# Moving 18 gathered dot products into the routing stage, and letting VectorE's weight remainders lead by two blocks

## The reference, cut to what matters

```python
def chunk_fn(hc):                                   # 128 tokens at a time
    q = (hc @ w_query).reshape(PEER_CHUNK, PEER_HEADS, PEER_KEY_DIM)     # 8 heads
    s1 = jnp.einsum('chk,nk->chn', q[..., :PEER_HALF_DIM], keys_1)       # 128 keys
    s2 = jnp.einsum('chk,nk->chn', q[..., PEER_HALF_DIM:], keys_2)
    v1, i1 = lax.top_k(s1, PEER_TOPK_HALF)                               # 16 of 128
    v2, i2 = lax.top_k(s2, PEER_TOPK_HALF)
    cand = (v1[..., :, None] + v2[..., None, :]).reshape(PEER_CHUNK, PEER_HEADS, -1)
    cand_idx = (i1[..., :, None] * N_KEYS + i2[..., None, :]).reshape(PEER_CHUNK, PEER_HEADS, -1)
    top_s, pos = lax.top_k(cand, PEER_TOPK)                              # 16 of 256
    experts = jnp.take_along_axis(cand_idx, pos, axis=-1)                # of 16384
    gate = jax.nn.softmax(top_s.astype(jnp.float32), axis=-1).astype(hc.dtype)
    u = jnp.take(expert_u, experts, axis=0)
    act = jax.nn.gelu(jnp.einsum('chkd,cd->chk', u, hc))
    v = jnp.take(expert_v, experts, axis=0)
    return jnp.einsum('chk,chkd->cd', gate * act, v)
```

## Time and profile before

| what | us |
|---|---|
| median of three runs (lowest, highest) | 2969.31 (2959.89, 2971.57) |
| the profiled execution, its own time | 2977.3 |
| its span in the trace | 2975.5 |
| PE busy | 2872.6 (97%) |
| DVE busy | 1737.5 (58%) |
| POOL busy | 1257.9 (42%) |
| ACT busy | 1114.3 (37%) |

### The profile page before, as it was taken

The page is one execution under the profiler, slowest core; times in us unless marked ns, Lnnn a source line. Parts: engine busy times, 40 slices in busy tenths (PEclk is TensorE's granted clock), DMA queues, the critical chain, the costliest instruction groups (busy, mean ns, idle before and its releaser), DMA issues. The chain is left out here.

```text
span 2975.5 us, 42156 instructions
## 1 busy us (share of the span) xinstructions
PE 2872.6 (97%) x14606; PEld 2452.6 (82%) x14606; DVE 1737.5 (58%) x2980; ACT 1114.3 (37%) x1499; POOL 1257.9 (42%) x1348
## 2 busy tenths in 40 slices
PE   7899999999999999999999999999996899999998
PEld 5777888877688878787789999999985799999997
DVE  7957555234445541797507995877732456666664
ACT  5554222236442223424334334656641223333332
POOL 2635777554157765686455775111100020122210
PEclk9999999999999999999999999999997999999999
DMA  8315555522045553232233555888872677788772
GB/s 335 120 37 212 197 191 167 159 87 89 27 137 197 193 177 109 86 102 72 84 105 113 157 155 161 289 285 283 284 250 80 222 265 269 273 289 289 274 258 83
DMA packets 184380, 532.75 MB, mean 179 GB/s; under 512 B 17376, under 2 KB 79584, under 8 KB 182496
## 3 DMA queue, kind: packets, MB, share of 16 engines
q1 hardware_dynamic: 143584, 402.44, 40.7%
q0 software_dynamic: 18432, 67.12, 7.1%
q10 hardware_dynamic: 22272, 61.98, 5.5%
HBM read 470.65 MB, written 60.82 MB: 179 GB/s over the span
## 5 line engine op out<-in xcount | busy, mean ns | idle before, releaser
L615 POOL TENSOR_TENSOR w_lo<-raw,w_hi 128x256 fp32r<-128x256 f32 x1216 | 1112.9, 948 | 729.0 <-ACT w_hi L652 727.9
L2000 PE MATMUL ps<-h_hi,w_hi 128*128 128x512 f32 (+1 forms) x2392 | 925.4, 387 | 51.4 <-DVE w_lo L1901 38.7
L2000 PE MATMUL ps<-h_hi,w_lo 128*128 128x512 f32 (+1 forms) x2392 | 914.9, 382 | 0.0
L2000 PE MATMUL ps<-h_lo,w_hi 128*128 128x512 f32 (+1 forms) x2392 | 893.9, 382 | 0.0
L652 ACT ACTIVATE w_hi<-raw 128x1024 fp32r<-128x1024 f32 x509 | 538.9, 1060 | 901.8 <-PE ps L2000 636.4
L2000 PEld LDWEIGHTS ps<-h_hi,w_hi 128*128 128x128 f32 x2392 | 455.6, 190 | 131.7 <-issue 50.8
L2000 PEld LDWEIGHTS ps<-h_hi,w_lo 128*128 128x128 f32 x2392 | 455.1, 190 | 69.9 <-issue 0.2
L2000 PEld LDWEIGHTS ps<-h_lo,w_hi 128*128 128x128 f32 x2392 | 455.2, 190 | 69.0 <-issue 0.7
L633 POOL DMA_INDIRECT t_row<-in_u_rows,t_ix x64 | 64.9, 1013 | 540.0 <-DVE t_dot L1908 535.1
L1901 DVE TENSOR_TENSOR w_lo<-raw,w_hi 128x1024 fp32r<-128x1024 f32 x200 | 243.6, 1219 | 52.0 <-ACT w_hi L652 50.5
L1263 DVE CUSTOM_DVE_ANT_0 ada<-ada,cvec 128x1024 f32<-128x1024 f32 x144 | 225.3, 1594 | 30.7 <-DMA ada<-in_ada 26.0
(11 more groups left out here) (384 smaller groups left out, 3850.1 us busy)
## 6 DMA issues: line engine op xcount, KB each, us to landing
ada<-in_ada SPq DMA_DIRECT2D x144, 512.0 KB, 3.6
raw<-in_expert_u SPq DMA_DIRECT2D x128, 512.0 KB
raw<-in_expert_v SPq DMA_DIRECT2D x128, 512.0 KB
raw<-in_ffn_in SPq DMA_DIRECT2D x88, 512.0 KB
expert_act<-g_act ACTq DMA_DIRECT2D x128, 224.0 KB, 4.2
gate_matrix<-w_st ACTq DMA_DIRECT2D x14, 2048.0 KB, 8.6
e_w<-gate_matrix SPq DMA_DIRECT2D x16, 1792.0 KB
e_g<-expert_act SPq DMA_DIRECT2D x128, 224.0 KB
```

The costliest lines, as they stand in the source:

```text
L615: last = nc.gpsimd.tensor_tensor(w_lo[:, k, c:c + 256], raw[:, k, c:c + 256], w_hi[:, k, c:c + 256].bitcast(F32), ALU.subtract)
L2000: return nc.tensor.matmul(out, a, b, start=start, stop=stop_)
```

## The change

It has four parts.

1. **Early dots.** The row numbers of the first 64 tokens are made right after tile 0 of the routing (those tokens lie in it). 18 of the 64 dots move into the routing: one follows every third step from step 24 on (`E_STEP`; tile 1 begins with step 23). Their gathers stand in POOL's program behind every second split, from U block 18 on (`E_BLOCK`), in three buffers `t_early` of their own. The transposes and the copy that make `t_h` move from U block 52 to behind U block 3. The routing loop is written out instead of looped.
2. **Fewer dots later.** In the gates stage 1/2 dot per block instead of 3/4, in the last 16 U blocks 1/2 instead of 1/4, the last 10 in the first 10 V blocks; V rows start at V block 16, 5/8 of one per block, fewer of them in the first block of a group.
3. **Remainders lead.** In the last 16 U blocks iteration b writes remainders up to block b+2 before it does `gated`; at the first V block of each group the remainder of the V block two ahead comes before `e_t`, and so do that iteration's dots and rows.
4. **SP.** The fourth V block's raw load and group 1's `e_w` stand before the wait for the last activations, and that `e_w` waits only for the last `e_t` of group 0.

```diff
+EARLY, E_BLOCK, E_STEP = 18, 18, 24
+    t_early = [ar(f"t_early{i}", (8 + 4 * i) * K, [D]) for i in range(U_SLOTS)]
...
-        for k in range(2):
-            sp.wait_ge(act_st[k], ADA_ALL + 16 * NK // 2)
-        with sp.Fori(0, NG - 1) as g:
+        def group_step(g):
             for k in range(GE):
                 sp_raw(sp, (g * GE + (mv + k + 3), (mv + k + 3) % RING), A["expert_v"][g * GE + (k + 3), :, :], 1024)
                 if k == 0:
                     gates_in(g + 1)
+                    if isinstance(g, int):
+                        for b in range(2):
+                            sp.wait_ge(act_st[b], ADA_ALL + 16 * NK // 2)
                 group_in(g + 1, k)
+        group_step(0)
+        with sp.Fori(1, NG - 1) as g:
+            group_step(g)
...
-    V_DOTS = 32
+    V_DOTS = 16
+    SHARE = (0, 3, 4, 5, 6, 7, 8, 9)
+    def front(v):
+        return v // GE * GE + GE * SHARE[v % GE] / 10
     def dots_by(b):
-        if b < U_GATES:
-            return max(0, b) * 3 // 4
         if b < U_BLOCKS:
-            return U_GATES * 3 // 4 + (b - U_GATES) // 4
-        return min(ROWS, U_GATES * 3 // 4 + U_LAST // 4 + (b - U_BLOCKS) * 5 // 8)
+            return EARLY + max(0, b) // 2
+        return min(ROWS, EARLY + U_BLOCKS // 2 + int(front(b - U_BLOCKS)))
     def rows_by(v):
-        return min(ROWS, max(0, v - V_DOTS) * 3 // 4)
+        return min(ROWS, int(front(max(0, v - V_DOTS)) * 5 / 8))
...
+        pool.wait_ge(row_ready, 2)
+        for m in range(first * RING, gates):
             split(m, m % RING)
-        pool.wait_ge(row_ready, 2)
+            b = m - M0["expert_u"] - E_BLOCK
+            if b >= 0 and b % 2 == 0 and b // 2 < EARLY:
+                gather(b // 2)
+        pool.wait_ge(row_ready, 3)
         pool.wait_ge(rt_mm, 1)
+        for j in range(EARLY, ROWS):
+            gather(j)
...
         def step(ins):
             own_d.link(dve, ins)
+            taken["steps"] += 1
+            if taken["steps"] >= E_STEP and taken["steps"] % 3 == 0 and taken["dots"] < EARLY:
+                if taken["dots"] == 0:
+                    dve.wait_ge(row_ready, 2)
+                    dve.wait_ge(row_copied, 1)
+                dve_dot(dve, taken["dots"])
+                taken["dots"] += 1
...
-        with dve.Fori(0, TT) as i:
+        for i in range(TT):
...
+            if i == 0:
+                for a in range(PKS):
+                    rows, picks = slice(a * GT, (a + 1) * GT), slice(a * ROWS, (a + 1) * ROWS)
+                    last = v.scalar_tensor_tensor(out=t_dot[rows, :], in0=r_i[0:GT, 0, 0, picks], scalar=float(NK),
+                                                  in1=r_i[0:GT, 1, 0, picks], op0=ALU.mult, op1=ALU.add)
+                step(last)
+                v.tensor_copy(t_ix[:, :], t_dot[:, :]).then_inc(row_ready, 1)
...
-        for b in range(U_GATES, U_BLOCKS):
-            dve_remainder(dve, gates + b - 1)
-            if b == U_BLOCKS - GE:
+        def remainders(b):
+            while ahead[0] < b:
+                dve_remainder(dve, gates + U_GATES + ahead[0])
+                ahead[0] += 1
...
+        for b in range(U_LAST):
+            remainders(b + min(3, b + 1))
+            if b == U_LAST - GE:
...
+                def lead():
+                    remainders(U_LAST + n + 3)
+                def work():
+                    dots(U_BLOCKS + n)
+                    rows(n)
+                if k == 0:
+                    lead()
+                    work()
+                    gated(g + 1, k, (g + 1) % 2, lambda: None)
+                else:
+                    gated(g + 1, k, (g + 1) % 2, lead)
+                    work()
```

More of the change, by code:

```diff
@@ L556, in gates_in @@
         def gates_in(g):
-            if not isinstance(g, int):
+            if not isinstance(g, int) or g:
                 sp.wait_ge(wa_t, g * GE)
@@ L622, in pool_program, with gather @@
         gates = M0["expert_u"] + U_FIRST
-        with pool.Fori(2, gates // RING) as i:
+        first = (M0["expert_u"] + E_BLOCK) // RING
+        def gather(j):
+            if j >= U_SLOTS:
+                pool.wait_ge(row_used, j - U_SLOTS + 1)
+            nc.gpsimd.indirect_dma_start(out=row_slot(j)[:, :], out_offset=None, in_=A["u_rows"],
+                                         in_offset=bass.IndirectOffsetOnAxis(ap=t_ix[:, j:j + 1], axis=0))\
+              .then_inc(u_in[j % U_SLOTS], 16)
+        with pool.Fori(2, first) as i:
             for k in range(RING):
                 split(i * RING + k, k)
-        for m in range(gates // RING * RING, gates):
+        pool.wait_ge(row_ready, 2)
+        for m in range(first * RING, gates):
             split(m, m % RING)
-        pool.wait_ge(row_ready, 2)
+            b = m - M0["expert_u"] - E_BLOCK
+            if b >= 0 and b % 2 == 0 and b // 2 < EARLY:
+                gather(b // 2)
+        pool.wait_ge(row_ready, 3)
         pool.wait_ge(rt_mm, 1)
[L630 to L635, removed]
+        for j in range(EARLY, ROWS):
+            gather(j)
         pool.wait_ge(blk_done, M0["expert_v"])
@@ L1137, in act_peer @@
         four(0)
+        act.wait_ge(row_mm, 1)
+        nc.scalar.activation(t_h[:, :].rearrange("p (b n) -> p b n", b=2), pa[:, 0:2, :], ACT.Copy).then_inc(row_copied, 1)
         with act.Fori(1, U_FIRST // RING - 1) as i:
@@ L1819, in dve_router @@
         v = nc.vector
+        taken = {"steps": 0, "dots": 0}
         def step(ins):
             own_d.link(dve, ins)
+            taken["steps"] += 1
[5 more added lines that the diff above has]
+                taken["dots"] += 1
         def settle(ins):
@@ L1862, in dve_router @@
         v.tensor_tensor(e, e, bc(z1, 2, TK), ALU.mult).then_inc(gate_done, 1)
+        assert taken["dots"] == EARLY
         dve.wait_ge(gate_done, 1)
         for a in range(PKS):
[L1865 to L1870 removed]
+            last = v.tensor_copy(t_gate[a * GT:(a + 1) * GT, :], r_i[0:GT, 2, 0, a * ROWS:(a + 1) * ROWS])
+        last.then_inc(row_ready, 1)
         v.tensor_copy(iota_t[:, :, :], bc(iota, 2, 2))
@@ L1904, in dve_dot @@
     def dve_dot(dve, j):
-        row = t_row[j % U_SLOTS]
+        row = row_slot(j)
         dve.wait_ge(u_in[j % U_SLOTS], 16 * (j // U_SLOTS + 1))
@@ L2416, in pe_peer @@
         m, T = M0["expert_u"], T0["expert_u"]
-        with pe.Fori(0, U_FIRST // RING - 1) as i:
-            for k in range(RING):
-                first(m, T, k, i, RING)
+        for k in range(RING):
+            first(m, T, k, 0, RING)
         pe.wait_ge(row_ready, 1)
@@ L2423, in pe_peer @@
         last.then_inc(row_mm, 1)
+        with pe.Fori(1, U_FIRST // RING - 1) as i:
+            for k in range(RING):
+                first(m, T, k, i, RING)
         for k in range(U_FIRST - RING, U_FIRST - RING // 2):
```

67 lines of the change are left out of this document (28 added, 39 removed).

## The result

The changed kernel takes 2930.31 us (median of four runs, 2923.99 to 2934.16) against 2964.73 us for the kernel before (four runs, 2959.89 to 2971.57): ratio 0.988, 95% interval 0.9847 to 0.9913. That is 1.2% faster, by 34.4 us and clear of noise, inside the range of the forecast and 6.9 us above its 2923.4. The profiled execution took 2926.46 us with a span of 2924.7, 50.8 us less than the profiled one of before (2977.3).

A forecast was written before the change was run, and what follows sets the result against it. PE bounds the kernel, so time is won only where it idles or runs at its lower clock. -57.5 - 9.5 + 18.7 + 2.4 = -45.9 us from a median of 2969.3 gives 2923.4; own range 2911 to 2941, stated range 2905 to 2942.

The forecast's parts named there:

- Ring of U blocks 120 to 127: Waits circling remainder, PE, gelu, `wa_hi`, `wa_lo`; leading remainders open it, eight blocks take 39.0 us instead of 96.5: gain 57.5.
- Stage border: V group 0 takes 39.7 us instead of 49.2, with the remainder before `e_t` and `e_w` issued earlier: gain 9.5.
- Fewer dots in the gates stage: Gates stage: PE has no idle time there that a freer DVE could give back: 0 us.
- V rows per group: V stage: rows from block 16, 5/8 per block, and dots in the first V blocks cost 0 us.
- the slower rival: V groups: a row waiting for its gather delays `wa_lo` in 13 groups; 3 us past the slack gives 2994 us; 3%.
- Stall at the transposes: Routing's end: dots wait for gathers tied to PE, so PE stands still 18.7 us; floor 12.8, ceiling 25.
- POOL's lag: Splits 35 to 39: POOL falls 3 to 6 us behind, mostly made up before block 52; full at last gather 2929, 8%.
- Clock after the stall: PE restarts at the lower clock after standing still at the routing's end: loss 2.4 us, ends 0 and 5.
- The `t_h` transposes ahead of PE's loop: Transposes and copy moved ahead make block 52's split end 1 us later; no other cost counted.
- The rival without a stall: Routing's end: gathers land well ahead, 21.6 us of dots fit in 26.15 us of slack, time 2902 us; 5%.
- another wait takes the ring's place: U blocks 120 to 127: queued `e_g` loads or ACT's order keep half of the 67.0 us, time 2957; 7%.
- The rule of the Trainium skill: Two-input VectorE instructions and GpSimd SBUF reads exclude each other; each of 18 dots costs POOL up to its own length.

The follow-up runs named there:

- sp_old: `lead_only` with SP's wait for the last activations ahead of group 0 again, as before the change: median 2909.56 us, lowest 2903.07, ratio 0.9817.
- lead_only: Changed kernel without early dots (EARLY = 0), later dots and V rows spread as in the kernel before: median 2897.65 us, lowest 2896.02, ratio 0.9764.
- th_late: `lead_only` with the `t_h` transposes and ACT's copy behind U block 51 again, PE's loop from block 0: median 2894.81 us, lowest 2892.27, ratio 0.976.
- step30_block15: Changed kernel with early dots from routing step 30 instead of 24 and gathers from U block 15 instead of 18: median 2902.42 us, lowest 2899.01, ratio 0.9778.
- lead_one: `lead_only` with remainders in U blocks 112 to 127 one iteration earlier than before the change, instead of three: median 2908.49 us, lowest 2898.64, ratio 0.9806.
- th_late_peeled: `th_late` with PE's blocks 0 to 3 kept written out ahead of the loop: median 2892.59 us, lowest 2892.27, ratio 0.9751.
- vgather_late: `step30_block15` with POOL's wait for the first V gather 12 blocks later: median 2900.22 us, lowest 2896.42, ratio 0.9791.
- pe_shift: `lead_only` with the `t_h` transposes written four times ahead of PE's loop: median 2901.18 us, lowest 2898.32, ratio 0.9775.
- dots_only: Changed kernel without leading remainders and without SP's new order, early dots and their spread kept: median 2993.18 us, lowest 2986.48, ratio 1.0087.
- block15: Changed kernel with early gathers from U block 15 instead of 18: median 2914.02 us, lowest 2908.36, ratio 0.983.
- step30: Changed kernel with early dots from routing step 30 instead of 24: median 2908.68 us, lowest 2906.12, ratio 0.981.

## Why the prediction was right, and where it was off

The mechanism was right at both places. Measured between the two profiled executions:

- *Ring of U blocks 120 to 127*: forecast -57.5, measured 38.9 - 96.5 = -57.6. `wa_lo` still waits for `wa_hi` and harms nothing. Right; one iteration earlier would nearly do. (The prediction says that remainders are written two iterations earlier. It is three, as its "due three blocks later" has it; no number hangs on it.)
- *Stage border*: forecast -9.5. No gap at 2285.0, and no other wait before V block 11. Right; 4.2 us of it are SP's order (`sp_old`), the rest the remainder ahead of `e_t`.
- *Fewer dots in the gates stage*: forecast 0. PE is busy for 320.00 of 320.00 there. Right.
- *V rows per group*: forecast 0, wrong. I priced dots and rows by DVE's time and by the buffers, and did not ask when the first six gathers go out. With the dots spread anew, POOL comes to its V gathers at 2319.4 (before at 2447.5), 0.9 us behind SP's load of `e_w` for group 2. Price: 2.2 us of wait, and a granted clock of 0.98 over 2300 to 2400 us, about 0.02 x 97.8 = 2.0 us more. The V stage confirms it: 628.0 us against 623.9 without a stop. It resembles the slower rival that I gave 3%, in that V rows make a group late, but at one group instead of 13, and by gathers that delay `e_w` instead of a row that waits for its gather.
- *Stall at the transposes*: forecast 18.7, measured 20.1, the sum of two misses. The routing ended at 1864.4 instead of 1858.6, since I counted POOL's lag at the last gather, where it was made up. It counts at a tile's first dot, because from there DVE runs without slack: the 15th dot came at 1809.63 where my chain has 1802.1, the 18th 34.9 us later, as forecast (35.0). The lag was 9.7 us and not 3 to 6; 7.0 of it are POOL's own and 2.7 PE's slower pace. Against it, the steps behind the last dot took 1.7 us less, the table load lay in the wait, and PE arrived 3.2 us later than in the execution of before (1867.54 - 20.10 = 1847.44).
- *Clock after the stall*: forecast +2.4. From the transposes to the gelu of block 119 it is 2246.29 - 1867.54 = 378.8 us, before 2222.50 - 1844.21 = 378.3: +0.5 net. `lead_only`, which has no stop there, takes 377.4 us for the same work (2221.19 - 1843.79), so the lower clock cost about 1.4 us. The kernel before lost 0.9 us against `lead_only` in this stretch, by something that I can't name.
- *The `t_h` transposes ahead of PE's loop*: I had them at "1 us later" for POOL and nothing else. Their own time is the same at either place, but behind the new one each matmul of U blocks 4 to 53 takes 4.0 ns more: 24 x 50 x 4.0 ns = 4.8 us. From the first gelu of the U stage (1584.00, before 1585.74) to the place of the stop PE took 5.0 us longer (263.44 against 258.47); `lead_only` less `th_late` is 3.8 us between lowest times and 4.8 in the traces. This term was missing from the sum.

Added up without the V stage's interval: -57.6 - 9.5 + 5.0 + 20.1 + 0.5 + 2.2 + 2.0 = -37.3. With 11.6 us for the pace in the V stage and 1.7 for the earlier start this is -50.6, against -50.8 between the profiles. The lowest times of both kernels give 2923.99 - 2959.89 = -35.9, the highest 2934.16 - 2971.57 = -37.4. The forecast of -45.9 was 8.5 to 10 us too good; 5.0 of that lie in the U loop and 4.2 in V block 11. The change of the medians, -34.4, misses it by 11.5. That the median of after lies only 6.9 above the forecast's 2923.4 is luck: the 2969.3 that I started from lay in the upper group of times, and four executions of before have a median of 2964.73. The stall came out near its forecast (20.1 for 18.7) by luck too, since its errors of 5.8 us late against 1.1 and 3.2 early nearly cancel.

The rival without a stall (5%) fell, and `step30_block15` shows what it lacked: the reason I gave against it, gathers tied to PE's pace, is what three blocks and six steps undo. That another wait takes the ring's place (7%) fell as well.

The rule of the Trainium skill (SBUF — State Buffer, section "SBUF: two separate sides") points the right way for POOL's stretch: two splits beside DVE's two-input work and dots took 13.39 us, against 5.64 for two undisturbed. It gives no size for the lag, and my 3 to 6 us from rows of before were too low.

What stays open: why 4.0 ns, and why a stop or a set of transposes sets the slower pace in one case and not in another.

## What to carry to other kernels

An in-order ring is opened by writing the producer one iteration ahead of the wait that it stood behind; more lead than one iteration brought at most 2.6 us here, between lowest times. Don't cut it too fine, though: a stop of 0.4 us in a stream of matmuls was followed by a slower pace that cost 12. Work that "fits into the slack" fits only if it waits for nothing: a chain with transfers woven in runs at the pace of their issues, so ask for each of them what its issue stands behind, and count a lag where the chain waits, not at its end. When one stage's work is made to end sooner, look for what that releases in a burst, and which load is due at that moment.

## What the runs showed of the hardware that was not expected

A 448-column matmul with its weight load has two intervals, 202.7 and 206.7 ns, both at granted clock 1.00, and keeps to one for hundreds of us ("short" and "long" below). In the V stage it was 206.7 in the profiled execution of before and 202.7 in that of after, without any difference in the code of PE there:

```profile
2400.00:2900.00 500.00, 500.00 (x2422) 454.07 (x2421) 315.61 (x386) 157.59 (x203) 87.23 (x71) 1.00 0.80 275
```

```profile
2400.00:2900.00 500.00, 500.00 (x2473) 464.01 (x2472) 308.36 (x362) 158.62 (x202) 62.69 (x54) 1.00 0.73 250
```

4.0 ns on all 3072 matmuls would be 12.3 us. Measured, the V stage takes 623.9 us without a stop at the short interval and 635.5 at the long one (`lead_one`), 11.6 more, about the distance between the two groups of times that most kernels here show (before: 2957.7 to 2963.9 and 2969.0 to 2973.6; `lead_only`: 2896.0 to 2899.1 and 2908.9). In the U loop all ten profiled kernels with transposes ahead of it have the long interval there, and the three without (the kernel before, `th_late`, `th_late_peeled`) the short one.

In the V stage the interval turns as well, and in all 13 profiles only where PE's stream has stopped. From U block 112 on four have no stop, and all four keep the short interval (`vgather_late`, `th_late`, `th_late_peeled`, `pe_shift`). Nine have at least one. Six of them turn long right behind a stop and stay so: the kernel before in the ring, `dots_only` at its last wait (2401 us), `lead_one` at U block 121, `lead_only` at V block 3, `block15` and `step30_block15` at the wait in V block 11. Three stay short behind theirs (the changed kernel, `step30`, `sp_old`). A stop can be too small for the list of PE's waits. This is `lead_only`'s, in the timeline of PE's weight loads:

```profile
2274.77 0.19 PEld L2060 LDWEIGHTS pa<-wa_hi,w_hi 128*128 128x128 f32 x1 [0.49 <-DVE w_lo L1939]
```

So the same wait of 2.4 us in V block 11 cost 4 us in `step30` and nearly 15 in `block15` (V stage 628.2 and 638.6 us, without a stop 623.9). This is also a likely source of the two groups of times: `th_late` and `th_late_peeled`, whose profiles show no stop, have nine times within 5.7 us. The executions that were not profiled can't confirm it, and one of `vgather_late`'s, at 2909.53, looks like the upper group all the same. Which way a stop turns the interval, I could not tell. For reading two profiles: compare the count of matmuls in equal busy windows before putting a difference of spans down to the change.
